# State-space stage: near products in four pieces, later weight splits, inside weights one slab earlier

## The reference, cut to what matters

```python
u = (h @ w_in)                                  # 256 x 1024
bu = einsum('gpc,bkgc->bkgp', bb, u_c)          # drive of the states, bb complex
x[t] = a * x[t-1] + bu[t]                       # complex, a per state
y = real(einsum('gcp,bkgp->bkgc', c, x)) + d_skip * u
y = gelu(y);  y = y * sigmoid(y @ w_glu)
return y @ w_out
```

## Time and profile before

| | |
|---|---|
| median of three runs | 1154.8 us (1152.64, 1154.8, 1155.75) |
| the profiled execution | 1149.64 us, of which the span of the core is 1147.8 us |
| mean granted clock | 0.994 |
| PE busy | 1103.6 us, 96% (7984 matmuls and as many weight loads) |
| DVE busy | 783.9 us, 68% |
| ACT busy | 592.1 us, 52% |
| POOL busy | 107.1 us, 9% |
| chain that ended last | PE 80%, DVE 11%, ACT 5%, issue 2%, POOL 1% |
| code fetched | 63 packets, 1.03 MB (queue "q8 instruction") |

### The profile page before, as it was taken

How to read it: one execution, slowest core, us unless ns; L and a number is a source line. 1 busy time by engine, 2 the same in 40 slices (tenths; PEclk the granted TensorE clock), 3 DMA queues, 4 the chain that set the end, 5 groups by cost and what they waited for, 6 DMA issues and landing times.

```text
span 1147.8 us, 19160 instructions
## 1 busy us (share of the span) xinstructions
PE 1103.6 (96%) x7984; PEld 928.2 (81%) x7984; DVE 783.9 (68%) x1276; ACT 592.1 (52%) x919; POOL 107.1 (9%) x114
## 2 busy tenths in 40 slices
PE   7999999999999999999998999999999899999997
PEld 6877878777899998887877887878878788888786
DVE  5747874768687874658566896887578767555553
ACT  6566533244565553465655664445673267345441
POOL 0405050600000000000000000013103100000000
PEclk9999999999999999999999999999999899999999
DMA  8533322024555555555323654555541245655561
GB/s 310 188 112 127 129 75 75 21 65 156 189 179 184 182 186 188 182 168 195 119 89 110 244 190 154 184 194 191 168 145 58 76 165 186 190 179 193 189 201 56
DMA packets 49671, 177.55 MB, mean 155 GB/s; under 512 B 5648, under 2 KB 6288, under 8 KB 49328
## 3 DMA queue, kind: packets, MB, share of 16 engines
q1 hardware_dynamic: 49440, 175.79, 46.4%
q10 hardware_dynamic: 144, 0.52, 0.1%
HBM read 175.25 MB, written 1.05 MB: 154 GB/s over the span
## 4 chain that ended last, share of the span: by engine, by line
PE 80%; DVE 11%; ACT 5%; issue 2%; POOL 1%; DMA 0%; SPq 0%; DVEq 0%; ACTq 0%
PE wps L2810 19%; PE wps L2812 19%; PE wps L2811 19%; PE tps L2799 4%; PE wps L2832 3%; PE wps L2830 3%; PE wps L2831 3%; DVE wlo L1918 3%; PE tps L3248 1%; ACT whi L1507 1%; PE tps L3068 1%; DVE arena L2140 1%; PE tps L3073 1%; PE tps L2884 1%; PE tps L3045 1%
## 5 line engine op out<-in xcount | busy, mean ns | idle before, releaser
L1918 DVE TENSOR_TENSOR wlo<-raw,whi 128x1024 fp32r<-128x1024 f32 (+1 forms) x322 | 390.1, 1231 | 169.1 <-ACT whi L1507 167.9
L1507 ACT ACTIVATE whi<-raw 128x1024 fp32r<-128x1024 f32 (+1 forms) x322 | 326.9, 1052 | 82.0 <-PE wps L2812 79.1
L2810 PE MATMUL wps<-whi,a_hi 128*128 128x512 f32 (+1 forms) x864 | 345.0, 399 | 2.3 <-DVE a_lo L1926 1.5
L2812 PE MATMUL wps<-wlo,a_hi 128*128 128x512 f32 (+1 forms) x864 | 336.6, 390 | 0.0
L2811 PE MATMUL wps<-whi,a_lo 128*128 128x512 f32 (+1 forms) x864 | 336.0, 389 | 0.0
L2810 PEld LDWEIGHTS wps<-whi,a_hi 128*128 128x128 f32 x864 | 163.0, 189 | 38.8 <-issue 5.3
L2812 PEld LDWEIGHTS wps<-wlo,a_hi 128*128 128x128 f32 x864 | 162.7, 188 | 34.6
L2811 PEld LDWEIGHTS wps<-whi,a_lo 128*128 128x128 f32 x864 | 163.4, 189 | 31.0
L2810 PE MATMUL wps<-whi,f_hi 128*128 128x512 f32 x264 | 103.2, 391 | 0.0
L2812 PE MATMUL wps<-wlo,f_hi 128*128 128x512 f32 x264 | 102.8, 389 | 0.0
L2811 PE MATMUL wps<-whi,f_lo 128*128 128x512 f32 x264 | 102.7, 389 | 0.0
(11 more groups left out here) (434 smaller groups left out, 1311.4 us busy)
## 6 DMA issues: line engine op xcount, KB each, us to landing
raw<-in_w_dn SPq DMA_DIRECT2D x22, 512.0 KB, 3.3
raw<-in_w_0dn SPq DMA_DIRECT2D x22, 512.0 KB, 3.2
raw<-in_w_1dn SPq DMA_DIRECT2D x22, 512.0 KB, 3.3
raw<-in_w_ua SPq DMA_DIRECT2D x20, 512.0 KB, 3.3
raw<-in_w_ub SPq DMA_DIRECT2D x20, 512.0 KB, 3.4
raw<-in_w_0ug SPq DMA_DIRECT2D x20, 512.0 KB, 3.4
raw<-in_w_0uu SPq DMA_DIRECT2D x20, 512.0 KB, 3.3
raw<-in_w_1ug SPq DMA_DIRECT2D x20, 512.0 KB, 3.7
```

The costliest lines, as they stand in the source:

```text
L1507: activate(t.whi[n % NH][:, 0:w], t.raw[n % NR][:, 0:w], ACT.Copy).then_inc(m.done(s.act_hi, "hi", n), 1)
L1918: V.tensor_tensor(t.wlo[n % NR][:, 0:w], t.raw[n % NR][:, 0:w], t.whi[n % NH][:, 0:w].bitcast(F32), ALU.subtract).then_inc(m.done(s.dve_lo ...
L2810: T.matmul(o, xh, wh, start=first, stop=False)
L2812: mm = T.matmul(o, xh, wl, start=False, stop=last)
```

## The change

Four edits, all in the order of the list; no arithmetic is added or taken away.

1. The first `b_turn` (with its ACT copy) is emitted after the last j = 0 slab of si0, and so every later step of `local_weights` one slab sooner: k_build 3 and k_table 1 now stand after the last slab of si0.
2. `s5_near` takes a list of tiles. The first half runs as [0] before the second transposes, [1, 2] behind them, [3] behind drive 1; the second half as [4, 5] behind s5_far 0 and [6, 7] between the first two slabs of sg0.
3. The two rotations behind the scan are a piece of their own, `s5_back`; scan 4 is emitted ahead of parts 0 and 1, back 4 behind them.
4. One split moves from ahead of parts 0 to behind states 4, the next from ahead of states 5 to behind states 7, and the look-ahead is off (`ahead`) while the first slabs of sg0 and sg1 go through, so that two splits stand behind states 7 and the rest behind parts 3.

```diff
@@ order_of_work
+    ahead = [True]
...
-            while at["split"] <= min(n + LOOK, len(SLABS) - 1):
+            while (ahead[0] or at["split"] <= n) and at["split"] <= min(n + LOOK, len(SLABS) - 1):
                 split_next()
...
-    background.append(local_weights())
-    banks = whole(stream("si0", 8, main, {(0, 2): lambda b_, f=second: f()}))
+    local = local_weights()
+    background.append(local)
+    banks = whole(stream("si0", 8, main, {(0, 2): lambda b_, f=second: f(), (0, 3): lambda b_: next(local)}))
...
-    def near(m_, banks):
+    def near(m_, banks, kts):
         y_banks[m_] = banks
-        emit("s5_near", m_, [b.name for b in banks], [b.free for b in banks])
+        emit("s5_near", m_, [b.name for b in banks], [b.free for b in banks], kts)
...
-    near(0, si_banks)
+    near(0, si_banks, [0])
     u_t[1].extend(heads_T("h", "uT", 8, us_ready, kbs=[2, 3]))
+    near(0, si_banks, [1, 2])
+    emit("s5_back", 0)
     emit("s5_states", 0)
     emit("s5_scan", 1)
     emit("s5_decay", 3)
     drive(1)
+    near(0, si_banks, [3])
+    emit("s5_back", 1)
     emit("s5_states", 1)
...
     emit("s5_far", 0, [b.name for b in y_banks[0]])
-    near(1, banks)
+    near(1, banks, [4, 5])
...
-    split_next()
+    emit("s5_scan", 4)
     parts(0)
     parts(1)
-    emit("s5_scan", 4)
     emit("s5_decay", 6)
+    emit("s5_back", 4)
     emit("s5_states", 4)
+    split_next()
     emit("s5_scan", 5)
     emit("s5_decay", 7)
-    split_next()
+    emit("s5_back", 5)
     emit("s5_states", 5)
     sg = [stream("sg0", 8, main, banks=si_banks)]
+    ahead[0] = False
     next(sg[0])
+    near(1, banks, [6, 7])
     next(sg[0])
     emit("s5_scan", 6)
+    emit("s5_back", 6)
     emit("s5_states", 6)
...
     emit("s5_scan", 7)
+    emit("s5_back", 7)
     emit("s5_states", 7)
     next(sg[1])
+    ahead[0] = True
+    split_next()
+    split_next()
     emit("s5_far", 1, [b.name for b in y_banks[1]])
@@ vector_program
+    @part
+    def s5_back(n):
+        a, z, _, cosines, sines, _ = s5_unit(t, n)
+        dve.wait_ge(*m.at("scanned", n))
         V.tensor_tensor(a, z, cosines, ALU.mult).then_inc(m.done(s.dve_out, "back_re", n), 1)
@@ tensor_program
-    def s5_near(m_, banks, freed):
+    def s5_near(m_, banks, freed, kts):
...
-        for kt in range(4 * m_, 4 * m_ + 4):
+        for kt in kts:
```

More of the change, by code:

```diff
@@ L1142, in order_of_work @@
     emit("s5_decay", 4)
+    emit("s5_back", 2)
     emit("s5_states", 2)
@@ L1145, in order_of_work @@
     emit("s5_decay", 5)
+    emit("s5_back", 3)
     emit("s5_states", 3)
@@ L2565, in s5_scan @@
     def s5_scan(n):
-        a, z, flat, cosines, sines, _ = s5_unit(t, n)
+        flat = s5_unit(t, n)[2]
         dve.wait_ge(*m.at("s5_added", n))
@@ L2571, in s5_scan @@
             m.done(s.dve_out, "scanned", n), 1)
-        after_last()
+    @part
+    def s5_back(n):
+        a, z, _, cosines, sines, _ = s5_unit(t, n)
+        dve.wait_ge(*m.at("scanned", n))
         V.tensor_tensor(a, z, cosines, ALU.mult).then_inc(m.done(s.dve_out, "back_re", n), 1)
```

## The result

| | before | after |
|---|---|---|
| median | 1154.12 us (1148.84 to 1159.11, 20 runs) | 1156.68 us (1152.83 to 1162.91, 20 runs) |
| ratio | | 1.0037, 95% interval 1.002 to 1.0055 |
| the profiled execution | 1149.64 us, span 1147.8 | 1160.66 us, span 1158.9 |
| mean granted clock of it | 0.994 | 0.985 |

What follows compares the result with a forecast made beforehand. TensorE was taken as the bound, with only holes and slow stretches to win, in a race with DVE in the state-space stage. Terms -4.9 and +1.75 summed to -3.2: 1154.8 to 1151.6 us, range 1148.9 to 1154.6.

Steps and rivals of the forecast that it cites:

- the working of edit 1: Inside weights a slab sooner: drive 0 starts later through ACT's queue and the uT wait, +1.75 us (+1.0 to +1.9).
- A: Rival: the clock falls in the new 2.6 us hole ahead of k_build 0, loss 1.5, giving 1153.1; chance 0.19.
- E: Rival: the clock falls in k_build 0's new hole and stays low longer, +4.5 at 9 us, giving 1156.1; chance 0.10.
- The hole ahead of k_build 0: PE reaches k_build 0 a slab earlier but still waits for ACT's copies: idle grows from 1.21 to about 2.6 us.
- C: Rival: k_build 0's hole is not ACT's, so the move costs only up to 0.3, giving 1150.2; chance 0.12.
- Drive 1 sooner behind drive 0: With near pieces around the second transposes, drive 1 comes some 19.2 us after drive 0, formerly 20.8.
- D: Rival: near pieces don't make drive 1 sooner; DVE keeps its 1.38 and PE its hole, giving 1153.0; chance 0.09.
- s5_far 1 itself: At the full clock its matmuls take 4.14 plus a 1.7 code stop: 5.85 us in place of 6.43.
- B: Rival: the code stop doesn't come in s5_far 1 (4.14 us), -1.7 more, giving 1149.9; chance 0.13.
- Edits 2 to 4 together: Near pieces, reordered scan and moved splits end s5_far 1 at 912.4 instead of 917.3: -4.9 us.
- the clock has no cause to fall: With the 3.26 us hole ahead of s5_far 1 down to nothing or 0.3, s5_far 1 starts at about 906.6.
- The carried difference: The profiled execution, 1149.64, lies 5.2 us under the median; the forecast carried that over from 1146.4 to 1151.6.

Runs made afterwards that it cites:

- e10: The whole change plus 8 throw-away transposes on PE ahead of drive 0's wait for uT; 1152.28 us, ratio 1.0001 to the kernel before.
- e1: The whole change run again with no edit; 1156.49 us, ratio 1.005 to the kernel before.
- e5: The kernel before with two of the four ACT copies of c_spread 2 done twice, nothing reordered; 1152.02 us, ratio 1.0009.
- e12: The kernel before with only the earlier b_turn and inside weights, plus 8 and 6 throw-away transposes ahead of drives 0 and 1; 1152.13 us, ratio 0.9995.
- e2: The whole change without the earlier b_turn and inside weights; 1148.72 us, ratio 0.9976 to the kernel before.
- e8: The kernel before with only the first half of s5_near cut in three pieces; 1152.92 us, ratio 0.999.
- e7: The whole change with b_turn and inside weights at their old slabs, and c_spread 2 one slab earlier; 1147.32 us, ratio 0.9963 to the kernel before.
- e4: The whole change with c_spread 2's copies put ahead of the first b_turn on ACT; 1148.87 us, ratio 0.999 to the kernel before.
- e9: The whole change plus 20 throw-away transposes on PE ahead of k_build 0's wait; 1154.58 us, ratio 1.0024 to the kernel before.
- e3: The kernel before with only the earlier b_turn and inside weights; 1166.87 us, ratio 1.013.
- e11: The kernel before with only the earlier b_turn and inside weights, plus 20 throw-away transposes ahead of k_build 0; 1162.14 us, ratio 1.0042.

## Why the prediction was wrong

**The step that failed** is the end of the working of edit 1: "the wait for the uT copies (1.09 behind the transposes), which lay under k_build 3, is late next with 0.8." I saw that one wait ahead of drive 0 takes the place of another, and priced it as time on PE alone. It measured 1.09, 0.17 more than the wait it replaced, and behind it the granted clock falls in the drive: 6.3 us. With 0.85 of that wait filled the mean clock loss is back at the level of the kernel before (e10). The sum had no term for the clock in the drive, and no rival had it. Both rivals on the clock, A and E, put the fall into the new hole ahead of k_build 0, the largest idle time that the change makes. There the clock was full in the profiles of after and e1, and e5, with a hole of 2.39 in the old order, has the loss of the kernel before. E had the right sign, a size not far off (9 us of low work, +4.5; it was 13.7 us low and +6.3) and by luck nearly the right time, 1156.1, but the wrong place, and 0.10 was too little for it. A fall right behind that hole does exist: in the profile of e12 the clock is 0.66 from 845 to 850 and k_build 0 takes 1.17 in place of 0.87.

What spoke for it stood in the rows. The earlier trace rows have the clock falling 1.4 us behind an idle time of 1.29 (the mean of 0.71 puts the fall at 609.4), with PE busy all through (9 matmuls, 1.00 of 1.00 us), and I used them for the hole alone. A wait of about that size ahead of 256 small matmuls was in my own sum.

**Right, term by term** (times from the transposes of x on; before in the earlier trace rows):

- The hole ahead of k_build 0: forecast 2.6, measured 2.47 in the kernel after, and its releaser is ACT's copy of c_spread 2. So C (not ACT's hole) falls.
- Drive 0 later: forecast +1.75. It starts 865.95 - 844.68 = 21.27 behind the transposes of x, before 19.61: +1.66.
- Drive 1 sooner behind drive 0: forecast 19.2, measured 19.28 in e2, 19.27 in e8. So D (pieces don't work) falls.
- The rotations of unit 4: forecast 8.7 behind turn 4 (884.7 to 893.4), measured 909.02 - 900.27 = 8.75. The wait of 0.8 that I had put ahead of the rest of part 1 is there in e2, with 0.60 behind a scan of 1.21. In the kernel after the scan takes 1.83, and the rests follow each other (906.82, 2.28 for two).
- State 7: forecast 12.9 behind them, measured 922.3 - 909.02 = 13.3. PE has no hole left ahead of s5_far 1.
- s5_far 1 itself: forecast 5.85 with a stop of 1.7; measured 928.42 - 922.47 = 5.95 with a stop of 1.92. So B (no stop) falls. The stop came in all eight profiles of edits 2 to 4, 1.92 to 2.48. That it is code fits the trace: in each of the eight one packet of the queue "q8 instruction" starts between 0.54 us ahead of the stop and 0.10 behind its start (925.52 in the kernel after, where the stop is from 925.86 to 927.78). But such a packet came in the low burst of the kernel before too (914.09), where nothing stopped, and no run changed the code to try it. The rule of the Trainium skill (Runtime: NRT & Kernel Launch, section Instruction fetch mechanics) that such boundaries are mostly hidden doesn't hold for these bursts of small matmuls, if they are code.
- The stage behind s5_far 1 is only shifted in the kernel after: 230.5 us to the end, as before. In five of the other profiles of edits 2 to 4 it is not, see below.

**Mis-sized.** Edits 2 to 4 together: forecast -4.9, and e2's stage is 3.1 shorter. The rest is in two terms. Drive 1 takes 7.92 in place of 7.37 (54 and 202 matmuls with a stop "issue" of 0.23 between), and s5_far 1 takes 6.91, with the longest of the stops, 2.48, and 29 slow matmuls behind it (the clock is 0.71 from 914 to 918). In e7, where neither stop is that long, the stage is 4.7 shorter, 0.24 of it from drive 0. A third term I had put at nothing: "the clock has no cause to fall" once the hole of 3.26 is gone. In e2, e4, e7, e9 and e10 it falls all the same, 0 to 1.3 us behind the stop in s5_far 1, and stays low for 3.4 us, and from the end of s5_far 1 to the end of the span it is 231.6 to 232.1, not 230.5. So by the profiles e2 gains 2.0 and not 3.1. The ratio of e2 gives -2.8 (-5.3 to -0.2). In the kernel after, drive 1 runs from 891.68 to 900.2, 8.5 in place of 7.37, with two such stops: most of what its 77.4 lacks against the forecast's 79.1 - 3.2 = 75.9.

**Edit 1 by itself**: forecast +1.75, measured about +15 by the ratio. With the clock held in both drives (e12) the interval is 0.26% below to 0.16% above the kernel before, and +1.75 would be 0.15% above, just inside; the kernel before had more clock loss in that group of runs than in the others (11.7), which flatters e12. So a queueing cost of the size that I gave it is not ruled out, and nearly all of its price is the clock.

**The carried difference.** I carried the profiled execution's 5.2 us under the median over as a constant. Part of it is probably whether the low stretch at 230 us comes: of the 106 runs of the kernel before beside the experiments, 37 lie under 1150 us and 48 between 1153 and 1156, and the profiled one, under 1150, has no such stretch. That this is what parts the two heaps is not shown. That this shifted both kernels alike was an assumption; it did no harm that these runs show.

## What to carry to other kernels

Price a wait ahead of a long burst of small matmuls not by its own length alone but by the burst: at the low clock the drive took 11.62 in place of 7.37 and the products behind it 0.43 each in place of 0.23, here 6.3 us behind a wait of 1.09. When a move replaces one wait by another at such a place, fill it with PE work that has no cost of its own (a piece of the near products, as edit 2 does ahead of drive 1, or throw-away transposes), and compare the mean granted clock over many executions, since one profile can show either level. If a hole has a named copy at its end, look at what waits next before moving that copy: e7 closed a hole of 1.20 and had drive 0 only 0.24 sooner, for the next wait of 0.70.

## What I had not expected of the hardware

- The clock can fall inside work: in the kernel after at 868.5, 2.6 us into a drive in which PE has no hole, that is 2.6 behind the end of the wait of 1.09 and 16.4 behind that of the hole of 2.47. It stayed at 1.2 GHz for 13.7 us, with PE busy in all of them. In e1, e3 (both drives) and e11 it fell 2.5, 2.5, 2.6 and 1.9 us into the drive. In the kernel before it had fallen in the idle time itself, at 909.8 in the hole of 3.26.
- Eight throw-away transposes (0.85 us of PE) ahead of the drive lower the mean clock loss of the change from 13.8 to 8.6 us. Fourteen in e12 lower it from 24.0 to 8.8.
- Twenty transposes in the longer hole hardly change the mean in e9, 13.8 to 12.9, but spread it, 3.4 to 19.7; in e11 they take it from 24.0 to 14.7, with runs from 1.1 to 22.1.
- The "issue" stops in bursts of small matmuls go with the clock. s5_far 1 had none at the low level before and one of 1.92 to 2.48 at the full one in every profile of edits 2 to 4; s5_far 0 had one of 2.03 at the full level, and in e3, low for most of it, its 256 matmuls run through in 5.95 us. So going from the low to the full clock gives back 0.5 here (6.43 to 5.95), not 2.3.
